# A chunked delta rule in un-normalised form, with its inverse in three four-fold steps

## What is computed

```
q = l2norm(q) * HEAD_K ** -0.5;  k = l2norm(k)
G = cumsum(g);  decay[i, j] = exp(G[i] - G[j]) for i >= j, else 0
A = where(strict, beta * (k @ k.T) * decay, 0)
T = inverse(eye + A)
u = T @ (beta * v);  w = T @ (beta * exp(G) * k);  attn = (q @ k.T) * decay
per chunk: v_new = u - w @ S
           o = (q * exp(G)) @ S + attn @ v_new
           S = S * exp(G_last) + (k * exp(G_last - G)).T @ v_new
o = rmsnorm(o, onorm_g) * silu(z)
```

## Time and profile before

| what | value |
|---|---|
| median of 3 runs | 1364.1 us (1362.33 to 1373.99) |
| profiled execution | 1362.78 us, its span 1361.1 us |
| TensorE busy | 1212.0 us (89%), 8365 instructions |
| VectorE, ScalarE, GpSimd busy | 815.3, 625.3, 248.1 us |
| mean granted TensorE clock | 0.96 |
| moved by DMA | 206.87 MB, 152 GB/s on average |

### The profile page before, as it was taken

How to read it: one execution, slowest core, us unless ns; L and a number is a source line. 1 busy time by engine, 2 the same in 40 slices (tenths; PEclk the granted TensorE clock), 3 DMA queues, 4 the chain that set the end, 5 groups by cost and what they waited for, 6 DMA issues and landing times.

```text
span 1361.1 us, 21462 instructions
## 1 busy us (share of the span) xinstructions
PE 1212.0 (89%) x8365; PEld 1083.3 (80%) x8365; DVE 815.3 (60%) x943; ACT 625.3 (46%) x857; POOL 248.1 (18%) x198
## 2 busy tenths in 40 slices
PE   4989999999999999999998998998159999999980
PEld 4989999999999999999998998998145555555550
DVE  4437365384573753745736544523727989898865
ACT  4435343253343433523424322224236878787862
POOL 0001010010010100100101000000415565666633
PEclk9999999999999999999998998999579999999995
DMA  5271111111111211112110223484356999999976
GB/s 178 71 236 65 65 55 61 65 67 55 62 61 64 67 46 64 67 55 74 49 65 26 81 81 109 137 323 167 139 200 228 367 357 364 361 367 350 367 248 217
DMA packets 47574, 206.87 MB, mean 152 GB/s; under 512 B 5536, under 2 KB 8112, under 8 KB 35232
## 3 DMA queue, kind: packets, MB, share of 16 engines
q1 hardware_dynamic: 36256, 177.46, 36.5%
q10 hardware_dynamic: 8336, 18.62, 3.7%
q0 software_dynamic: 2928, 10.05, 2.1%
HBM read 175.48 MB, written 30.63 MB: 151 GB/s over the span
## 4 chain that ended last, share of the span: by engine, by line
PE 66%; DMA 13%; DVE 8%; ACT 6%; issue 4%; POOL 1%; SPq 1%; ACTq 0%; DVEq 0%; POOLq 0%
PE proj L627 25%; DMA gu_raw<-in_w_up 8%; PE proj L1347 5%; PE proj L994 5%; PE wideB L1368 5%; PE wideA L385 4%; PE proj L937 4%; PE wideB L377 3%; PE wideB L391 2%; DVE gu_lo L1425 2%; PE small L994 2%; DMA wraw<-in_w_in 2%; ACT gu_hi L1409 1%; POOL scr_rows L1841 1%; DMA staged<-scr_rows 1%
## 5 line engine op out<-in xcount | busy, mean ns | idle before, releaser
L627 PE MATMUL proj<-xnh,whi 128*128 128x288 f32 x1152 | 347.9, 302 | 11.6 <-DVE xnl L1927 7.2
L627 PE MATMUL proj<-xnl,whi 128*128 128x288 f32 x1152 | 347.3, 301 | 0.0
L627 PE MATMUL proj<-xnh,wlo 128*128 128x288 f32 x1152 | 347.0, 301 | 0.0
L627 PEld LDWEIGHTS proj<-xnh,whi 128*128 128x128 f32 x1152 | 218.0, 189 | 12.8 <-issue 6.5
L627 PEld LDWEIGHTS proj<-xnl,whi 128*128 128x128 f32 x1152 | 217.9, 189 | 0.0
L627 PEld LDWEIGHTS proj<-xnh,wlo 128*128 128x128 f32 x1152 | 217.8, 189 | 0.0
L1347 PE MATMUL proj<-gu_hi,xbh 128*80 128x512 f32 x256 | 105.0, 410 | 28.2 <-issue 19.1
L639 DVE TENSOR_TENSOR wlo<-wraw,whi 128x1024 fp32r<-128x1024 f32 x72 | 95.1, 1321 | 57.8 <-ACT whi L635 56.8
L1584 POOL TENSOR_TENSOR xbl<-xg,xbh 128x640 fp32r<-128x640 f32 x32 | 98.1, 3066 | 117.4 <-issue 115.6
L1437 DVE TENSOR_TENSOR d_lo<-d_raw,d_hi 128x2048 fp32r<-128x2048 f32 x32 | 110.4, 3451 | 3.8 <-ACT d_hi L1420 1.7
L1347 PE MATMUL proj<-gu_lo,xbh 128*80 128x512 f32 x256 | 102.6, 401 | 0.0
(11 more groups left out here) (341 smaller groups left out, 2544.5 us busy)
## 6 DMA issues: line engine op xcount, KB each, us to landing
wraw<-in_w_in SPq DMA_DIRECT2D x72, 512.0 KB, 3.4
gu_raw<-in_w_gate SPq DMA_DIRECT2D x32, 1024.0 KB, 7.4
gu_raw<-in_w_up SPq DMA_DIRECT2D x32, 1024.0 KB, 10.5
d_raw<-in_w_down SPq DMA_DIRECT2D x32, 1024.0 KB, 5.1
wraw<-in_w_out SPq DMA_DIRECT2D x24, 512.0 KB, 4.2
scr_y<-yout ACTq DMA_DIRECT2D x32, 320.0 KB, 7.1
scr_gate<-gate ACTq DMA_DIRECT2D x16, 288.0 KB, 2.1
staged<-scr_rows SPq DMA_DIRECT2D x9, 512.0 KB, 4.3
```

Source lines behind the costliest of these rows:

```text
L627: mm = pe.matmul(out, w[:, kc, :], x[:, kc, hh * HALF:(hh + 1) * HALF], start=(j == 0), stop=(j == 23))
```

## The change

The norms of q and k no longer enter q and k. The Gram products take the raw columns of q and k as they come out of the silu, so they aren't turned back. With c = beta / |k|^2 and r = v |k| - exp(G) (k @ S), both per row, the solve is made once per chunk on r, and its result is scaled by c. The norm of q goes into the output's root. The matrix is kept transposed. Its inverse starts from pairs and grows four-fold in each of three steps; a step is four dependent products (N, then three Horner sums) and, before it, one transpose with ScalarE's copy. Running sums come in rows: at the start they are turned once and written to DRAM (`scr_g`), and GpSimd's queue loads five rows per head, spread over the partitions (`grow`). Stream operands are cut to 64 rows or columns. Chunks of the scan take three positions. The loops over heads are written out on TensorE, VectorE and ScalarE; those of SP and GpSimd stay. Constants shrink from 12 to 8 squares.

In the diff's core, added lines of the delta rule stand alone where they replace what is printed above.

```diff
-LEVELS = 6
+STEPS = 3
...
+    scr_g = nc.dram_tensor("scr_g", (UNITS * HEADS, P), F32, kind="Internal").ap()
...
+        LEN = [P] * (UNITS - 1) + [STREAM]
+        V = [slice(u * P, u * P + LEN[u]) for u in range(UNITS)]
+        ROWS = [slice(0, LEN[u]) for u in range(UNITS)]
+        STEP_AT = (9, 14, 19)
+        SCAN_AT = 24
...
+        def held(k, part):
+            return UNITS - 1 if k == STEPS - 1 and part > 1 else UNITS
+        def of_chunk(c):
+            return [(UNITS - 1, Ss, 1), (0, Sp, 0)] if c == 0 else [(c, Sp, 0)]
         def gdn_tensor(pe, p, g):
             n = g + 1
+            q, k = silq[g % 2], silk[g % 2]
...
+            if p == 3:
+                pe.wait_ge(s["krest_set"], n)
+                for u in range(UNITS):
+                    mm = pe.matmul(wideB[ROWS[u], V[u]], k[:, V[u]], k[:, V[u]], start=True, stop=True)
+                mm.then_inc(s["kk_done"], 1)
+            if p == 5:
                 pe.wait_ge(s["v_scaled"], n)
                 for u in range(UNITS):
+                    mm = pe.matmul(wideA[ROWS[u], V[u]], k[:, V[u]], q[:, V[u]], start=True, stop=True)
+                mm.then_inc(s["kq_done"], 1)
...
+            for j in range(STEPS):
+                part = p - STEP_AT[j]
+                if not 0 <= part < 4:
+                    continue
+                if part == 0:
+                    pe.wait_ge(s["t_set"], STEPS * g + j + 1)
+                    if j == 0:
+                        pe.wait_ge(s["attn_set"], n)
                 else:
+                    pe.wait_ge(s["step_set"], 12 * g + 4 * j + part)
+                left, right = ((Bm, T), (N, M), (N, H), (N, H))[part]
+                place = (wideA, wideB)[part % 2]
+                for u in range(held(j, part)):
+                    mm = pe.matmul(place[ROWS[u], V[u]], left[ROWS[u], V[u]], right[ROWS[u], V[u]],
+                                   start=True, stop=True)
+                mm.then_inc(s["step_done"], 1)
+            if SCAN_AT <= p < SCAN_AT + 12:
+                c, part = divmod(p - SCAN_AT, 3)
+                if part == 0:
...
+                    u, state, o = of_chunk(c)[0]
+                    pe.matmul(small[ROWS[u], 2 * P * o:2 * P * o + P], k[:, V[u]], state[:, :], start=True, stop=True)
+                    pe.matmul(small[ROWS[u], 2 * P * o + P:2 * P * o + 2 * P], q[:, V[u]], state[:, :],
+                              start=True, stop=True).then_inc(s["ks_done"], 1)
+                elif part == 1:
+                    pe.wait_ge(s["r_set"], 4 * g + c + 1)
+                    pe.wait_ge(s["step_set"], 12 * n)
+                    for u, state, o in of_chunk(c):
+                        right = vr if u == 0 else rr
+                        left = H if u == UNITS - 1 else M
+                        mm = pe.matmul(wideA[ROWS[u], 512 + P * o:512 + P * o + P], left[ROWS[u], V[u]],
+                                       right[ROWS[u], U[u]], start=True, stop=True)
+                    mm.then_inc(s["y_made"], 1)
                 else:
+                    pe.wait_ge(s["z_set"], 4 * g + c + 1)
+                    for u, state, o in of_chunk(c):
+                        pe.matmul(wideB[ROWS[u], U[u]], attn[ROWS[u], V[u]], zz[ROWS[u], U[u]], start=True, stop=True)
+                        mm = pe.matmul(wideA[:, P * o:P * o + P], krest[ROWS[u], U[u]], zz[ROWS[u], U[u]],
+                                       start=True, stop=True)
                     mm.then_inc(s["kv_done"], 1)
+            if p == 41:
                 pe.wait_ge(s["o_scaled"], n)
                 for u in range(UNITS):
+                    mm = pe.transpose(wideA[:, V[u]], vn[ROWS[u], U[u]], ident[ROWS[u], ROWS[u]])
                 mm.then_inc(s["o_turned"], 1)
         def gdn_scalar(act, p, g):
             n = g + 1
             if p == 0:
                 act.wait_ge(s["qk_turned"], n)
+                if g == 0:
+                    act.wait_ge(s["rows_out"], 16)
                 wait(act, s["o_sum"], g)
+                act.activation(sq[:, 0:UW], wideA[:, 0:UW], ACT.Square)
+                act.activation(sq[:, UW:2 * UW], wideB[:, 0:UW], ACT.Square).then_inc(s["qk_square"], 1)
+            if p == 1:
+                act.wait_ge(s["gap_set"], n)
+                act.activation(Dm[:, :], Dm[:, :], ACT.Exp).then_inc(s["decay"], 1)
             if p == 3:
                 act.wait_ge(s["qk_sum"], n)
+                act.activation(st[:, 30:35], st[:, 5:10], ACT.Sqrt, bias=epsq[:, 1:2]).then_inc(s["k_root"], 1)
+            if p in (7, STEP_AT[0] + 4, STEP_AT[1] + 4):
+                done = STEPS * g + 1 + (0 if p == 7 else 1 if p < STEP_AT[1] else 2)
+                act.wait_ge(s["t_turned"], done)
+                place = wideB if p == 7 else wideA
+                act.activation(T[:, 0:TOK], place[:, 0:TOK], ACT.Copy).then_inc(s["t_set"], 1)
+            if SCAN_AT <= p < SCAN_AT + 12:
+                c, part = divmod(p - SCAN_AT, 3)
+                if part == 0:
+                    act.wait_ge(s["ks_done"], 4 * g + c + 1)
+                    act.wait_ge(s["r_set"], 4 * g + c + 1)
...
+                elif part == 1:
+                    act.wait_ge(s["y_made"], 4 * g + c + 1)
+                    for u, state, o in of_chunk(c):
+                        ins = act.activation(zz[ROWS[u], U[u]], wideA[ROWS[u], 512 + P * o:512 + P * o + P], ACT.Copy,
+                                             scale=st[ROWS[u], 25 + u:26 + u])
+                    ins.then_inc(s["z_set"], 1)
...
         def gdn_vector(dve, p, g):
             n = g + 1
+            if p == 0:
+                dve.wait_ge(gdec_set, n)
+                dve.wait_ge(s["grow_in"], 16 * n)
+                for u in range(UNITS):
+                    ins = dve.tensor_scalar(Dm[:, U[u]], grow[:, U[u]], gcur[:, KSUM, u:u + 1], 0.0, ALU.subtract,
+                                            ALU.min)
+                ins.then_inc(s["gap_set"], 1)
+                dve.wait_ge(s["qk_square"], n)
+                dve.tensor_tensor(units(krest[:, :]), units(wideB[:, 0:UW]), spread(KREST), ALU.mult)\
+                   .then_inc(s["krest_set"], 1)
             if p == 2:
+                dve.tensor_reduce(st[:, 0:10], units(sq[:, :]), X, ALU.add).then_inc(s["qk_sum"], 1)
+                dve.wait_ge(s["decay"], n)
+                dve.tensor_tensor(units(Dm[:, :]), units(Dm[:, :]), mask(C_UPPER), ALU.mult)\
+                   .then_inc(s["decay_cut"], 1)
+                dve.wait_ge(s["qk_sum"], n)
+                dve.tensor_scalar(st[:, 10:15], st[:, 5:10], EPS, None, ALU.add).then_inc(s["k_shift"], 1)
+                dve.tensor_scalar(st[:, 15:20], st[:, 0:5], EPS, EPS * P * P, ALU.add, ALU.mult)
+                dve.wait_ge(s["k_shift"], n)
+                dve.reciprocal(st[:, 20:25], st[:, 10:15]).then_inc(s["k_recip"], 1)
+                dve.wait_ge(s["k_recip"], n)
+                dve.tensor_tensor(st[:, 25:30], st[:, 20:25], gcur[:, KBETA, :], ALU.mult).then_inc(s["c_set"], 1)
+            if p == 4:
+                dve.wait_ge(s["k_root"], n)
                 dve.wait_ge(s["v_turned"], n)
+                dve.tensor_tensor(units(vr[:, :]), units(wideA[:, 0:UW]),
+                                  st[:, 30:35].unsqueeze(2).to_broadcast([P, UNITS, P]), ALU.mult)\
                    .then_inc(s["v_scaled"], 1)
+                dve.wait_ge(s["kk_done"], n)
                 dve.wait_ge(s["decay_cut"], n)
+                dve.wait_ge(s["c_set"], n)
+                for u in range(UNITS):
+                    ins = dve.scalar_tensor_tensor(Bm[:, U[u]], wideB[:, U[u]], st[:, 25 + u:26 + u], Dm[:, U[u]],
+                                                   ALU.mult, ALU.mult)
+                ins.then_inc(s["b_set"], 1)
+                dve.wait_ge(s["b_set"], n)
+                dve.tensor_tensor(units(M[:, :]), units(Bm[:, :]), mask(C_PAIR), ALU.mult).then_inc(s["m_cut"], 1)
+                dve.wait_ge(s["m_cut"], n)
+                dve.tensor_tensor(units(M[:, :]), units(M[:, :]), mask(C_ID), ALU.add).then_inc(s["m_set"], 1)
+            if p == 6:
+                dve.wait_ge(s["kq_done"], n)
+                dve.tensor_tensor(attn[:, :], wideA[:, 0:UW], Dm[:, :], ALU.mult).then_inc(s["attn_set"], 1)
+            for j in range(STEPS):
+                part = p - STEP_AT[j]
+                if not 0 <= part < 4:
+                    continue
+                dve.wait_ge(s["step_done"], 12 * g + 4 * j + part + 1)
+                w = min(held(j, part) * P, TOK)
+                if part == 0:
+                    ins = dve.tensor_tensor(units(N[:, :]), units(wideA[:, 0:UW]), mask(C_STEP + P * j), ALU.mult)
                 else:
+                    dst, src = ((H, wideB), (H, wideA), (M, wideB))[part - 1]
+                    ins = dve.tensor_tensor(dst[:, 0:w], M[:, 0:w], src[:, 0:w], ALU.add)
+                ins.then_inc(s["step_set"], 1)
+            if SCAN_AT <= p < SCAN_AT + 12:
+                c, part = divmod(p - SCAN_AT, 3)
```

(77 more changed lines are left out.)

300 lines of the change are left out of this document (83 added, 217 removed).

## The result

The changed kernel takes 1376.82 us (median of 20 runs, 1366.47 to 1387.99); the kernel before, run beside it on the same chip, 1370.76 (20 runs, 1359.76 to 1376.25). The ratio is 1.0052, with a 95% interval of 1.0027 to 1.0078. The forecast of 1312 missed by 65 us. The profiled execution took 1373.93 us (span 1372.3); before, 1362.78 (span 1361.1).

The account below looks back on a forecast made before the run. TensorE's own work was taken to bound the heads: 7 x -6.7 + 1 - 6.1 = -52 us from the profiled 1362.78 gives 1310.8; the median lies 1.3 above, so 1312 us, range 1298 to 1337.

Parts of the forecast that it names:

- Counts and prices of transposes and full products: TensorE's work per head: 44 fewer transposes give -4.4 us, 7 fewer products -1.5 us.
- the -0.8: Stream unit term: 12 fifth-unit products a head shrink from 128x128 to 64x64, -0.07 us each, -0.8 us a head.
- The chains of the steps and of the scan: Between TensorE's groups: a step's VectorE chain, 1.10 us, just fits under 8 projection products, 1.16; scan stages fit too.
- the rival of uncovered hand-offs: Twelve step hand-offs a head each wait out a 0.8 us convolution: 9.6 - 6.7 = 2.9 us more, 1387; chance 0.03.
- For head 0 rows_out adds a write and a read in series ... +1 us once: Opening of head 0: writing and reading back the rows before grow arrives costs 1 us, once.
- The landing: I take 2.8, nearer to the state load: Grow's transfer at a head's opening lands in 2.8 us, between state load 2.1 and gather 6.4, leaving 0.5 us slack.
- The rival "grow late": Grow lands 3.6 us later than taken, 3.1 beyond the slack, eight times: +25 us, 1337; chance 0.12.
- Head 7, "-6.1": Head 7's stage beside the first output product: 3 us wait at Gram q, but an earlier end under the fill; -6.1 us.
- the 0.4: Waits term in the sum a head: 0.4 us less TensorE waiting than the 0.8 before.
- The low end: Fast end of the range: stream unit at half and no waits give 1302, less 4 for head 7: 1298.
- no waits at all (-0.8 a head): Part of the range's fast end: TensorE's waiting vanishes entirely, -0.8 us a head.

Follow-up runs that it names:

- e3: Changed kernel with grow's load issued about a head earlier and the stream unit zero-padded to 128; 1312.98 us, ratio 0.961 to the kernel before.
- e9: Changed kernel with full-width stream unit, grow loaded early in 128 pieces, and the fill's first VectorE parts ahead of head 7's work; 1309.23 us, ratio 0.9581.
- e5: Changed kernel with grow loaded about a head earlier and each 64x64 product of the steps issued twice; 1364.21 us in one run.
- e7: Changed kernel with gates stored by head, so grow is 128 pieces of 2560 B instead of 640 of 512, issued as late; 1346.22 us, ratio 0.984.
- e2: Changed kernel with the stream unit zero-padded to 128 everywhere, grow's load still late; 1337.86 us, ratio 0.9779 to the kernel before.

## Why the prediction was wrong

- **Counts and prices of transposes and full products: right.** With the two losses undone (e3) the groups of a head take 22.5 us, against 28.5 before. The fifth unit is full there, so the forecast for it is without the -0.8: 28.5 - 5.5 = 23.0. The chains of the steps and of the scan were covered by 8 projection products, as worked out; the rival of uncovered hand-offs did not come.
- **That e3 lands on the forecast, 1313 against 1312, is in part luck.** Its inner periods are 82.7, where the forecast without the -0.8 is 84.2; its first is 89.7, 7.0 above them where 1 was allowed; and head 7's stage ends 4.3 us short of its gain. These errors and the missing -0.8 largely cancel, and the mean period of 83.6 holds the first two. Of the 1.5 by which the inner periods are shorter, 0.5 are the groups and 0.4 the waits, which went to nothing; the rest is not placed.
- **"For head 0 rows_out adds a write and a read in series ... +1 us once": failed.** It cost 7.0 in e3, a stall of 4.4 us and the half clock with it, and 2.6 in e9 (85.3 - 82.7), where the load is in 128 pieces.
- **"Stream unit. 12 products shrink, -0.8": the step that failed.** It measured +4.0. I priced the product, from a row with 40 *moving* columns, and took "nothing" for the worst bound. e5 shows the product at half, but 0.32 us beside it for each group of the steps that mixes the shapes. In the changed kernel 19 groups a head are narrow in part (two Grams, ten in the steps, four of transposes, three in the scan): a head's groups take 26.1 us for 22.5, and the projection product behind most of the 19 takes 0.02 longer, together 4.0, or 0.21 a group. The rows of the prediction have no full and small products in turn, so nothing there excluded a loss, and the range should have reached to one. The trace before has two such places that I didn't use. Its 48 products with 16 stationary columns (L824, up to 44.19) stand between full ones at 0.13 us from start to start, with their weights loaded ahead: no price. But behind its five transposes of 16 rows (L838, to 51.04) the projection product's load starts together with it, as in loss two:

```profile
51.18 0.19 PEld L627 LDWEIGHTS proj<-xnh,whi 128*128 128x128 f32 x1
51.18 0.40 PE L627 MATMUL proj<-xnh,whi 128*128 128x288 f32 x1
```
- **"The landing: I take 2.8, nearer to the state load": failed.** It measured 6.9, above even the gather's 6.4. I reasoned that rows alike in length would land alike on DMA engines mostly idle; e7 shows that the number of pieces decides most of it (64 KB in 128 pieces 2.1, 320 KB in 128 pieces 3.7, in 640 pieces 6.9). The rival "grow late" had the mechanism at 3.1 us a head; 3.5 came in the mean and 4.2 in the inner heads, some of it half clock, which I had in no term. Alone it would have meant some 1337: e2 has 1337.86. I gave it 0.12, and nothing to both failing together.
- **Head 7, "-6.1": half failed.** The stage took 94.8 us, 93.4 before, 87.3 forecast, and 91.6 in e3. The narrow unit explains 3.2 of it. Of the 4.3 left, a part is the half clock after the 5.2 us stall. Before, it covered 3.5 us of TensorE's work after the stall; in e3 it lasts from the stall's end at 690.1 to 697.0. From 692.2 on:

```profile
692.20:697.00 4.80, 4.77 (x21) 4.80 (x22) 4.77 (x4) 1.11 (x1) 0.00 (x0) 0.50 0.00 0
```

Gram k falls into it (1.99 us for 1.04), where before only projection did so. The rest are waits in the steps and the scan behind VectorE's mixes:

```profile
PE wideA L402 <- DVE rr L526: 1.6, 2, 0.9
PE wideB L380 <- DVE H L519: 0.9, 1, 0.9
```

- **Sum of the miss**, 1373.93 - 1310.8 = 63 us: periods 637.3 - 7 x 83.4 = 53.5, of which 1 was allowed for the first head; head 7's stage 7.5; the first opening 2.9 earlier; everything behind the stage 6.0 later. 52.5 - 2.9 + 7.5 + 6.0 = 63. Of the 52.5, 52.0 are what e3 takes out of the seven periods (637.3 - 585.3). The last term is not settled: the expert products last 326.0 us from first to last here, 321.1 before, and between 320.5 and 325 in experiments that leave that code alone.
- **The low end** of the range had an error of its own: "no waits at all (-0.8 a head)" counts twice the 0.4 that the sum a head had already taken, so 1302 should read some 1306. Nothing hangs on it.

## What to carry to other kernels

A smaller tile is not a smaller cost when it stands in a queue of full ones: price the change of shape, both ways, before the product, and where neighbours are full size, padding may win (here by 4.0 us a head). Price a transfer by its pieces as well as its bytes, and issue it as soon as its buffer is free, since everything in the waiting engine's queue stands behind it. A stall of TensorE of 2.3 to 3.0 us was followed by half clock in some heads, 1.5 us more; put both into one term. And look at the first period and the inner ones apart: a mean over seven hid a start-up cost of 7.0 us here.

## What was not expected of the hardware

- A group of four full 128x128 fp32 products with a fifth of 64x64 costs 0.32 us more than its products; with one of 64 rows and 128 columns 0.38, if that product itself takes 0.21.
- At each change of shape that cost time the weight load started together with its product (212.57 and 212.82), and between equals 0.11 to 0.14 us ahead. The opening *transposes* with 128 rows and 64 columns had it ahead and cost nothing more (ten in 1.01 us, with and without the narrow unit). In the scan, products with the state of the same 128 rows and 64 columns cost 0.58 us for 0.36. The 16-column products of the kernel before, next to full ones, cost nothing more either. What decides which shapes pay stays open.
- An extra 64x64 product in a row of its like costs 0.11 us.
- 320 KB in 640 pieces of 512 B kept the DMA engines 84% busy at 79 GB/s, in 128 pieces of 2560 B 87% at 230 GB/s. 64 KB issued behind the 640 pieces landed in 6.1 us instead of 2.1.
- Half clock followed three of the six stalls of 2.3 to 3.0 us in the changed kernel and two of six of 2.2 to 2.4 us in e2; every stall of 4.4 us or more ahead of Gram k in the first head met it (seven traces), and the one where head 7 opens (4.8 us before, 5.2 after) in all thirteen.
